# Decayed keys of a gated recurrence: turned on TensorE, or in 32x32 blocks on VectorE with 16 transfers per head

## The chip, the cores and the metric

One core of a Trainium2 chip runs the whole program in one launch. The metric is the device time of one execution in microseconds (us). Engines are called PE (TensorE; PEld is its weight load), DVE (VectorE), ACT (ScalarE), POOL (GpSimd) and SP (SyncE). All times on the profile are counted from the start of the span.

## The reference, cut to what matters

Two layers with RMSNorm and residual work on x of 512 x 1024 in float32. Layer 1 is an HGRN2 recurrence with 16 heads of 128 features, in chunks of 32 steps; layer 2 is dilated attention, and a final RMSNorm closes. The change touches layer 1 alone:

```python
q, f_pre, i_in, gate = u @ w_in        # four projections, 1024 -> 2048 each
f = lb + (1 - lb) * sigmoid(f_pre); k = 1 - f; b = cumsum(log f)     # in a chunk of 32
scores = causal((q * exp(b)) @ (k * exp(-b)).T)
o = scores @ v + (q * exp(b)) @ state
state = exp(b_last) * state + (k * exp(b_last - b)).T @ v
y = o * rsqrt(mean(o*o) + eps) * norm_g * silu(gate); h = x + y @ w_out
```

The kernel carries the state over blocks of 128 steps, of which there are four, so three blocks of keys decayed to the end of their block ("end-weighted keys", `kend`) are multiplied with the values.

## The kernel before, in words

Activations lie with features on the partitions and the 512 steps in the row. A large product is split in high and low parts of float32r: three matmuls of 512 columns for each block of 128 inputs (`split_matmuls`, L534). Weight tiles (512 KB) come through four slots: SP loads a tile once the slot's earlier tile has been split into its high part (ACT, `split_hi`, L955) and its low part (DVE, `split_lo`, L1342), each done when PE has finished the tile that held the slot (`load_after`, L365). Products land in three PSUM banks in turn.

Layer 1 goes over four quads of four heads (`quads`). In a quad PE works through three weight tiles for each head h: forget gate F, query Q and output gate G. Each tile is two halves of twelve 512-column matmuls. Between the halves the inner work of the head before is put in by a list (`recurrence`, called with `half` 0 to 5). For the last head of a quad it stands between the halves of the value products, or in the last quad between the columns of the out-projection. The order before is:

- after half 0, `scores`: 16 score products (L747, each two records), then, once `kend` is ready, the turning of `kend`: four products with the identity for block 1 (L752, each two records, into reversed strips of 32 partitions) and two transposes (L755) for blocks 0 and 2, into PSUM;
- after half 1, `updates`: three products of turned keys and values (L765), once ACT has copied PSUM to `kT` (`kT_copy`, L1110);
- after half 2, `outputs`: scores by values and state by queries (L776, L779), once DVE has masked the scores (L1493) and made the states (`states`, L1500 to L1503);
- after half 3, `norm_sum` (L786, L787): the sum of squares of the output, once ACT has squared it (L1115, L1117) and DVE has made its low part (`osq_low`, L1556).

DVE's order for head h is written out by hand in its `hg_body`: `gate` and `mask_scores` of the head before, the bound of F's exponent, `states` of the head before, `forget` (L1510), `cumulate` (L1518), `split_lo` of F, `osq_low` and `hg_output` (L1560, L1561) of the head before, then `decays` of this head: L1529 to L1550, with `kend` written at L1547 and signalled by `kend_ready`; then `split_lo` of Q, `y_low`, `bound_gate`, `split_lo` of G. ACT's order mirrors it: `kT_copy` of the head before, the sigmoid of F, `split_hi` of F, log (L1150), `square` of the head before, exp(b) (L1154), `out_rstd`, exp(-b) (L1158), `split_hi` of Q, `y_high`, exp of G (L1164), `split_hi` of G, `sigmoid` (L1132, L1134).

POOL first adds biases to a table for layer 2 (`bias_runs`, L453, 55 small instructions, with the value moves of the prologue, L444, in their middle), stores the table to DRAM and expands it there (L457 to L468), loads the first bias tiles (L430, L432), and only then enters `hg_body`, in which it moves value strips (`turn_chunks`, L444). In layer 2 POOL makes 16 transfers for each head to move 32x32 blocks between strips of partitions (`move_blocks`, L508), after DVE has turned them (L1754).

Of the kernel before, what the change touches and what calls it, by code (L numbers as in the profile page):

```python
# [30 lines left out]
F32 = mybir.dt.float32  # L31
# [101 lines left out]
def program(nc, x, ln_g, hg_w_in, hg_lb, hg_norm, hg_w_out, at_w_in, at_w_out, rel_bias, final_g,  # L133
            consts, classes, relmask, out):
    ctx = ExitStack()
    with ctx:
# [39 lines left out]
        rows = sb("rows", [P, 10, S])  # L176
        ef, fg, kk, lnf, bb, eb, enb, kend, spare_row, sT = [rows[:, i, :] for i in range(10)]

# [3 lines left out]
        aft = sb("aft", [P, S])  # L182
        kT = sb("kT", [P, ST - 1, P])
        state = sb("state", [P, ST - 1, P])
# [82 lines left out]
        q_ready, keys_ready, scores_done, sT_ready = sems("q_ready keys_ready scores_done sT_ready")  # L267
        kend_ready = sem("kend_ready")
        kT_done, kT_ready, U_done, state_ready = sems("kT_done kT_ready U_done state_ready")
        squared, osq_hi_ready, osq_ready = sems("squared osq_hi_ready osq_ready")  # L270
# [20 lines left out]
        def head(q, h):  # L291
            return q * HQ + h

        def quads(eng, body):
# [58 lines left out]
        def _(sp):  # L353
# [50 lines left out]
            for layer in (HG, AT):  # L404
                for n in range(layer.pro):
                    load_after(layer, None, n, False)

                def body(q, last):
                    for n in range(layer.quad_tiles(last)):
                        load_after(layer, q, n, last)  # L410
                quads(sp, body)

# [13 lines left out]
        def _(pool):  # L426
# [21 lines left out]
            for n, (g, bucket, first, count) in enumerate(runs):  # L448

                if n == len(runs) // 2:  # L450
# [3 lines left out]
                                              relb_sb[:, bucket * GROUPS + g:bucket * GROUPS + g + 1], None, ALU.add)  # L454
            ins.then_inc(ext_ready, 1)
            pool.wait_ge(ext_ready, 1)
            pool.dma_start(ext_dram.rearrange("g h e -> h g e"),  # L457
# [15 lines left out]
            load_bias(0)  # L473

            def hg_body(q, last):
                if not last:
                    turn_chunks(q)
            quads(pool, hg_body)

# [49 lines left out]
        def _(pe):  # L529
# [228 lines left out]
            def updates(g, h):  # L758

                if h == 0:  # L760
                    for turned in v_turned:
                        pe.wait_ge(turned, (g // HQ + 1) * 16 * NC)
                pe.wait_ge(kT_ready, g + 1)
                for b in range(ST - 1):
                    ins = nc.tensor.matmul(p_U[:, b * P:(b + 1) * P], kT[:, b, :], v_sb[0][:, b, h * P:(h + 1) * P],  # L765
                                           start=True, stop=True)
                ins.then_inc(U_done, 1)
# [32 lines left out]
            def hg_body(q, last):  # L800
                for h in range(HQ):
                    for half in range(2 * HG.per_head):
                        head_tile(HG, q, HG.per_head * h + half // 2, half % 2, first=(h == 0 and half < 2))
                        if h:
                            recurrence(head(q, h - 1), h - 1, half)
                for half in range(KT):
                    if last:
                        out_column(HG, q, HG.heads + half // 2, HG.heads + half, half, range(HQ - 1))
                    else:
                        values(HG, q, 0, half // 2, half % 2)  # L810
                    recurrence(head(q, HQ - 1), HQ - 1, half)
                out_projection(HG, q, last)
# [134 lines left out]
        def _(act):  # L947
# [160 lines left out]
            def kT_copy(g):  # L1108
                act.wait_ge(kT_done, g + 1)
                nc.scalar.activation(kT[:, :, :].rearrange("p a b -> p (a b)"), p_kT[:, 0:(ST - 1) * P], ACT.Copy)\  # L1110
                    .then_inc(kT_ready, 1)

            def square(g):
                act.wait_ge(O_done, g + 1)
                nc.scalar.activation(enb[:, :], p_O[:, :], ACT.Square).then_inc(squared, 1)  # L1115
                act.wait_ge(squared, g + 1)
                nc.scalar.activation(osq["hi"], enb[:, :], ACT.Copy).then_inc(osq_hi_ready, 1)  # L1117

# [17 lines left out]
            def hg_body(q, last):  # L1136
                for h in range(HQ):
                    g, before = head(q, h), head(q, h - 1) if h else None
                    number, bank, _ = HG.event(q, 3 * h + F_)
                    if h:  # L1140
                        kT_copy(before)
# [8 lines left out]
                    nc.scalar.activation(lnf[:, :], fg[:, :], ACT.Ln).then_inc(lnf_ready, 1)  # L1150
                    if h:
                        square(before)
                    act.wait_ge(b_ready, g + 1)
                    nc.scalar.activation(eb[:, :], bb[:, :], ACT.Exp).then_inc(eb_ready, 1)  # L1154
                    if h:
# [4 lines left out]
                    if h:  # L1160
                        y_high(before, h - 1)
# [8 lines left out]
                square(g)  # L1170
                if not last:
# [163 lines left out]
        def _(dve):  # L1335
# [184 lines left out]

            def decays(link, q, h, g, low_before):
                number, bank, _ = HG.event(q, 3 * h + Q_)
# [10 lines left out]
                if low_before:  # L1533
# [20 lines left out]
            def osq_low(g):  # L1554
                dve.wait_ge(osq_hi_ready, g + 1)
                nc.vector.tensor_tensor(osq["lo"], enb[:, :], osq["hi"].bitcast(F32), ALU.subtract).then_inc(osq_ready, 1)  # L1556

# [59 lines left out]
            def hg_body(q, last):  # L1617
# [9 lines left out]
                for h in range(HQ):  # L1627
                    g, before = head(q, h), head(q, h - 1) if h else None
                    if h:
                        gate(HG, q, h - 1, before, 3 * (h - 1) + G_)  # L1630
                        mask_scores(before)
# [12 lines left out]
                    early = last and h == HQ - 1  # L1644
# [17 lines left out]
                osq_low(g)  # L1662
                if last:
# [261 lines left out]
```

## Time and profile before

| | |
|---|---|
| median of 3 runs | 1588.45 us (1588.4 to 1588.81) |
| the profiled execution: its own time | 1588.76 us |
| its span, first to last instruction | 1587.1 us |
| around the span | 1.66 us |
| granted TensorE clock, mean | 0.999 of full |
| last `kend` product of layer 1 on PE | at about 492 us |

The profile gives busy time by engine, the chain that ended last, groups of instructions, and, on request, every instruction in order of time. In the timelines a row is the start in us, the length in us, the engine, the line, the operation and what it writes and reads, with a count where several are merged; idle time of the engine before it stands in brackets. Matmuls are pipelined, so the distance between two starts, not the length shown, is what a matmul takes from PE.

### The profile page before, as it was taken

What the parts mean: (1) busy time and instruction counts of PE and PEld (TensorE: products, weight loads), DVE (VectorE), ACT (ScalarE), POOL (GpSimd) and SP (SyncE); (2) the same over time, 40 slices, a digit from 0 to 9 for tenths busy, and PEclk for the clock granted to TensorE, in tenths of its full rate; (3) what the DMA queues carried; (4) which work ended last, traced back from release to release, by engine and by line L of the source; (5) the groups of instructions that cost most, each with busy time, mean ns of one, the idle gap of its engine ahead of it and who ended that gap; (6) DMA issues with size and microseconds to landing.
All of it is one profiled execution on the core that took longest, in us unless ns stands there. A gap on an engine that the chain in (4) does not pass through costs nothing.

```text
span 1587.1 us, 23898 instructions
## 1 busy us (share of the span) xinstructions
PE 1579.5 (100%) x8731; PEld 1306.9 (82%) x8731; DVE 807.4 (51%) x1415; ACT 633.3 (40%) x1078; POOL 360.2 (23%) x694
## 2 busy tenths in 40 slices
PE   9999999999999999999999999999999999999998
PEld 8888888888887888888888888888888888888887
DVE  7874675585577733444333444433245441434445
ACT  6553453454354533333232343322343332233333
POOL 5601000000000082222173211248022225502210
PEclk9999999999999999999999999999999999999999
DMA  6623223223321353444344433425344434534421
GB/s 194 201 80 112 79 79 106 81 78 99 100 73 48 120 152 98 111 106 112 91 140 114 117 93 97 104 91 165 86 106 112 116 78 132 144 89 110 111 73 67
DMA packets 268164, 169.23 MB, mean 107 GB/s; under 512 B 60032, under 2 KB 240848, under 8 KB 268080
## 3 DMA queue, kind: packets, MB, share of 16 engines
q1 hardware_dynamic: 204448, 138.75, 31.0%
q0 software_dynamic: 21488, 28.24, 5.9%
q10 hardware_dynamic: 42144, 1.05, 1.5%
q8 instruction: 61, 1.00, 0.3%
q14 instruction: 23, 0.19, 0.0%
HBM read 144.37 MB, written 5.71 MB: 95 GB/s over the span
## 4 chain that ended last, share of the span: by engine, by line
PE 99%; DVE 1%; ACT 0%; issue 0%; POOL 0%; ACTq 0%; POOLq 0%
PE proj L534 84%; PE inner L534 3%; PE inner L908 2%; PE inner L903 2%; PE inner L861 1%; PE inner L842 1%; PE inner L776 1%; PE inner L779 1%; PE inner L747 1%; PE inner L765 1%; PE inner L857 0%; PE inner L755 0%; PE proj L680 0%; PE inner L786 0%; PE inner L695 0%; PE inner L787 0%
## 5 line engine op out<-in xcount | busy, mean ns | idle before, releaser
L1342 DVE TENSOR_TENSOR w_lo<-raw,w_hi 128x1024 fp32r<-128x1024 f32 x252 | 307.3, 1220 | 476.3 <-ACT w_hi L955 473.1
L534 PE MATMUL proj<-u_hi,w_hi 128*128 128x512 f32 x1280 | 505.9, 395 | 0.2 <-issue 0.2
L534 PE MATMUL proj<-u_hi,w_lo 128*128 128x512 f32 x1280 | 498.9, 390 | 0.0
L534 PE MATMUL proj<-u_lo,w_hi 128*128 128x512 f32 x1280 | 498.8, 390 | 0.0
L955 ACT ACTIVATE w_hi<-raw 128x1024 fp32r<-128x1024 f32 x252 | 265.4, 1054 | 192.0 <-PE proj L534 131.3
L534 PEld LDWEIGHTS proj<-u_hi,w_hi 128*128 128x128 f32 x1280 | 240.4, 188 | 53.7 <-issue 5.0
L534 PEld LDWEIGHTS proj<-u_hi,w_lo 128*128 128x128 f32 x1280 | 240.2, 188 | 51.3
L534 PEld LDWEIGHTS proj<-u_lo,w_hi 128*128 128x128 f32 x1280 | 240.6, 188 | 48.2
L508 POOL DMA_DIRECT2D rows<-qx x240 | 117.7, 498 | 253.6 <-DVE qx L1754 251.3
L534 PE MATMUL proj<-w_hi,u_hi 128*128 128x512 f32 x440 | 173.6, 394 | 0.0
L534 PE MATMUL proj<-w_hi,u_lo 128*128 128x512 f32 x440 | 171.5, 390 | 0.0
L534 PE MATMUL proj<-w_lo,u_hi 128*128 128x512 f32 x440 | 171.3, 389 | 0.0
L1280 ACT ACTIVATE qk<-proj 128x512 f32<-128x512 f32 x96 | 57.0, 594 | 242.3 <-PE proj L534 242.3
L488 POOL DMA_DIRECT2D v<-qk x192 | 100.3, 529 | 55.5 <-PE inner L908 54.3
L1206 ACT ACTIVATE rows<-rows,negm 128x160 f32<-128x160 f32 (+2 forms) x128 | 56.7, 444 | 140.4 <-DVE negm L1714 140.4
L534 PE MATMUL proj<-y_hi,w_hi 128*128 128x512 f32 x248 | 97.1, 391 | 0.7 <-DVE sg L1479 0.4
L534 PEld LDWEIGHTS proj<-w_hi,u_hi 128*128 128x128 f32 x440 | 82.6, 188 | 17.6 <-DVE w_lo L1342 0.9
L534 PEld LDWEIGHTS proj<-w_hi,u_lo 128*128 128x128 f32 x440 | 82.6, 188 | 17.5
L534 PE MATMUL proj<-y_hi,w_lo 128*128 128x512 f32 x248 | 96.6, 389 | 0.0
L534 PEld LDWEIGHTS proj<-w_lo,u_hi 128*128 128x128 f32 x440 | 82.7, 188 | 16.8 <-issue 0.2
L534 PE MATMUL proj<-y_lo,w_hi 128*128 128x512 f32 x248 | 96.5, 389 | 0.0
L430 POOL DMA_DIRECT2D bias_n<-bias_tiles x16 | 9.0, 562 | 345.7 <-DVE rows L1704 335.2
(214 smaller groups left out, 1657.1 us busy)
## 6 DMA issues: line engine op xcount, KB each, us to landing
raw<-at_w_in SPq DMA_DIRECT2D x160, 512.0 KB, 4.3
raw<-hg_w_in SPq DMA_DIRECT2D x63, 512.0 KB, 4.0
rows<-qx POOLq DMA_DIRECT2D x240, 44.0 KB, 2.4
raw<-hg_w_out SPq DMA_DIRECT2D x16, 512.0 KB, 3.5
raw<-at_w_out SPq DMA_DIRECT2D x16, 512.0 KB, 5.1
v<-rows POOLq DMA_DIRECT2D x64, 64.0 KB, 2.3
v<-qk POOLq DMA_DIRECT2D x192, 16.0 KB, 3.4
v<-x SPq DMA_DIRECT2D x4, 512.0 KB, 6.3
```

What stands on the lines that cost most here:

```text
L488: pool.dma_start(v_sb[2][own:own + STEPS, r, :], staged(q, 2, s)[c * RES + r::CLASSES * RES, :]).then_inc(v_moved[s], 16)
L508: pool.dma_start(pT_far[j * CH:(j + 1) * CH, i, :, :], turned[i * CH:(i + 1) * CH, j, :, :])\
L534: ins = nc.tensor.matmul(bank[:, :], stationary(a), moving(b), start=(first and n == 0), stop=(last and n == 2))
L747: ins = nc.tensor.matmul(to, aft[:, b * P + c * CH:b * P + (c + 1) * CH], q_steps(b, 0, c, NC - c), start=True, stop=True)
L765: ins = nc.tensor.matmul(p_U[:, b * P:(b + 1) * P], kT[:, b, :], v_sb[0][:, b, h * P:(h + 1) * P], start=True, stop=True)
L776: ins = nc.tensor.matmul(p_O[:, s], v_sb[0][:, b, h * P:(h + 1) * P], sT[:, s], start=True, stop=(b == 0))
L903: nc.tensor.matmul(p_O[:, c * P:(c + n) * P].rearrange("p (t i n) -> p t i n", t=n, n=CH), v_sb[0][:, c, h * P:(h + 1) * P], tiles(2 * c, ...
L908: ins = nc.tensor.matmul(by_class[:, r], v_sb[c][:, r, h * P:(h + 1) * P], tiles(i, 1)[:, 0], start=False, stop=(i == len(TILES) - 1), ski ...
L955: nc.scalar.activation(w["hi"][:, slot, :], raw[:, slot, :], ACT.Copy).then_inc(hi_ready, 1)
L1206: nc.scalar.activation(probs[:, i, 0:n], probs[:, i, 0:n], ACT.Exp, bias=negm[:, i:i + 1], accum_out=stat[:, i // ST, 1, b:b + 1]).then_in ...
L1280: nc.scalar.activation(o, src, ACT.Copy, scale=QSCALE if i in (Q0, Q1, Q2) else 1.0)\
L1342: nc.vector.tensor_tensor(w["lo"][:, slot, :], raw[:, slot, :], w["hi"][:, slot, :].bitcast(F32), ALU.subtract).then_inc(w_ready, 1)
```

## The change: what it does

For 14 of the 16 heads (all but the last two of the last quad) DVE turns `kend` in 32x32 blocks (two transpose instructions, `turn_keys`), into a spare row of the work area. Sixteen transfers of 32 partitions x 384 B each then move the blocks to their strips of `kT`: eight from POOL's queue, eight from SP's. PE leaves out the eight L752 and two L755 records for these heads. `updates`, `outputs` and `norm_sum` are put one half later for them, and wait for both groups of transfers. `kT` is laid out with the three blocks innermost, so that the stationary operand of L765 is read with a step of three elements, for all 16 heads. The square goes to `tmp` in place of `enb`, exp(-b) goes ahead of the square on ACT, and on DVE `decays` and `split_lo` of Q go ahead of `hg_output`. POOL's part of layer 1 goes ahead of the storing of the bias table. For the last two heads the order is as before.

```diff
-        kT = sb("kT", [P, ST - 1, P])
+        kT = sb("kT", [P, P, ST - 1])
+        keys_of = lambda b: kT[:, :, b]
...
+        OWN_KEYS = 2
+        def by_transfer(last, h):
+            return not (last and h >= HQ - OWN_KEYS)
+        def square_of(transfer):
+            return tmp[:, 0, :] if transfer else enb[:, :]
+        def move_strips(eng, to, moved):
+            for c in to:
+                for i in range(NC):
+                    eng.dma_start(kT[c * CH:(c + 1) * CH, i * CH:(i + 1) * CH, :],
+                                  turned_keys[i * CH:(i + 1) * CH, c, :, :]).then_inc(moved, 16)
...
                     for n in range(layer.quad_tiles(last)):
                         load_after(layer, q, n, last)
+                        h = (n - SLOTS) // HG.per_head
+                        if layer is HG and n - SLOTS == h * HG.per_head and 0 <= h < HQ and by_transfer(last, h):
+                            wait_turn(sp, sp_met, keys_turned, head(q, h) + 1)
+                            move_strips(sp, range(NC // 2, NC), keys_high)
...
+            def move_keys(q, h):
+                wait_turn(pool, pool_met, keys_turned, head(q, h) + 1)
+                move_strips(pool, range(NC // 2), keys_low)
+            def hg_body(q, last):
+                for h in range(HQ):
+                    if by_transfer(last, h):
+                        move_keys(q, h)
+                if not last:
+                    turn_chunks(q)
+            quads(pool, hg_body)
             pool.wait_ge(ext_ready, 1)
...
-            def scores(g):
+            def scores(g, transfer):
...
                 ins.then_inc(scores_done, 1)
+                if transfer:
+                    return
                 pe.wait_ge(kend_ready, g + 1)
...
-                pe.wait_ge(kT_ready, g + 1)
+                if transfer:
+                    pe.wait_ge(keys_low, 8 * NC * NC * (g + 1))
+                    pe.wait_ge(keys_high, 8 * NC * NC * (g + 1))
+                else:
+                    pe.wait_ge(kT_ready, own_keys(g))
...
-            def recurrence(g, h, half):
+            def recurrence(g, h, half, transfer):
+                late = 1 if transfer else 0
                 if half == 0:
-                    scores(g)
-                elif half == 1:
-                    updates(g, h)
-                elif half == 2:
+                    scores(g, transfer)
+                elif half == 1 + late:
+                    updates(g, h, transfer)
+                elif half == 2 + late:
                     outputs(g, h)
-                elif half == 3:
+                elif half == 3 + late:
                     norm_sum(g)
...
                     nc.scalar.activation(enb[:, :], bb[:, :], ACT.Exp, scale=-1.0).then_inc(eb_ready, 1)
+                    if late:
+                        square(before, True)
                     split_hi(HG, q, 3 * h + Q_, last)
-                    if h:
+                    if late:
+                        out_rstd(before)
+                    if soon:
                         y_high(before, h - 1)
...
                     split_hi(HG, q, 3 * h + G_, last)
-                    if h == HQ - 1:
+                    if late:
+                        y_high(before, h - 1)
+                    if h == HQ - 1 and not by_transfer(last, h):
                         kT_copy(g)
                     sigmoid(g)
...
+            def turn_keys(g):
+                dve.wait_ge(kend_ready, g + 1)
+                blocks = kend.rearrange("p (b q n) -> p b q n", q=NC, n=CH)
+                nc.vector.transpose(turned_keys[:, :, :, 0:ST - 1:2].rearrange("p q n b -> p b q n"), blocks[:, 0:ST - 1:2, :, :])
+                last_first = bass.AP(turned_keys.tensor, turned_keys.offset + (NC - 1) * (ST - 1) * CH + 1,
+                                     [list(turned_keys.ap[0]), [-(ST - 1) * CH, NC], [ST - 1, CH]])
+                nc.vector.transpose(last_first, blocks[:, 1, :, :]).then_inc(keys_turned, 1)
...
                     .then_inc(kend_ready, 1)
+                if transfer:
+                    turn_keys(g)
...
                     if h:
-                        osq_low(before)
+                        osq_low(before, late)
+                    if soon:
                         hg_output(link, before)
...
-                    decays(link, q, h, g, early)
+                    decays(link, q, h, g, soon, by_transfer(last, h))
                     split_lo(HG, q, 3 * h + Q_, last)
-                    if h and h < HQ - 1:
-                        y_low(before, h - 1)
+                    if late:
+                        hg_output(link, before)
                     bound_gate(g)
                     split_lo(HG, q, 3 * h + G_, last)
-                    if h == HQ - 1 and not early:
+                    if late:
                         y_low(before, h - 1)
```

## Rows read from the trace of the kernel before

**Rows 1.** The page: busy time of the engines, and the chain that ended last.
```profile
PE 1579.5 (100%) x8731; PEld 1306.9 (82%) x8731; DVE 807.4 (51%) x1415; ACT 633.3 (40%) x1078; POOL 360.2 (23%) x694
...
PE 99%; DVE 1%; ACT 0%; issue 0%; POOL 0%; ACTq 0%; POOLq 0%
```

**Rows 2.** Timeline of PE, inner work of the first head, and the next scores.
```profile
54.38 0.77 PE L747 MATMUL inner<-qx,aft 128*32 128x128 f32 x32
54.96 0.40 PE L752 MATMUL inner<-ident,rows 128*32 128x128 f32 x8
...
55.49 0.48 PE L534 MATMUL proj<-u_hi,w_hi 128*128 128x512 f32 x1
...
58.35 0.83 PE L765 MATMUL inner<-v,kT 128*128 128x128 f32 x6
...
61.79 0.60 PE L776 MATMUL inner<-rows,v 128*128 128x128 f32 x4
...
66.12 0.39 PE L786 MATMUL inner<-osq_hi,ones_r 128*128 128x512 f32 x1
...
74.83 0.77 PE L747 MATMUL inner<-qx,aft 128*32 128x128 f32 x32
```

**Rows 3.** Timeline of PE in layer 2, products of 32-column tiles, then the projection.
```profile
602.75 0.86 PE L842 MATMUL inner<-qk 128*32 128x160 f32 x20
603.55 0.50 PE L534 MATMUL proj<-u_hi,w_hi 128*128 128x512 f32 x1
```

**Rows 4.** Timeline of DVE, between the first and the second head.
```profile
60.22 0.35 DVE L1503 SCALAR_TENSOR_TENSOR state<-state,tail,inner 128x128 f32<-128x128 f32 x1
61.19 0.55 DVE L1510 TENSOR_SCALAR rows<-rows,oml,lb 128x512 f32<-128x512 f32 x1 [0.62 <-ACT rows L1147]
...
62.52 1.22 DVE L1518 TENSOR_TENSOR_SCAN rows<-restart,rows 128x512 f32<-128x512 f32 x1 [0.33 <-ACT rows L1150]
...
64.85 0.69 DVE L1556 TENSOR_TENSOR osq_lo<-rows,osq_hi 128x512 fp32r<-128x512 f32 x1
...
69.68 0.68 DVE L1529 TENSOR_TENSOR qx<-proj,rows 128x512 f32<-128x512 f32 x1
...
73.66 0.68 DVE L1547 TENSOR_TENSOR rows<-aft,tail 128x512 f32<-128x512 f32 x1
```

**Rows 5.** Timeline of ACT, the square of the first head's output.
```profile
63.55 0.60 ACT L1115 ACTIVATE rows<-inner 128x512 f32<-128x512 f32 x1 [1.06 <-PE inner L779]
64.18 0.64 ACT L1117 ACTIVATE osq_hi<-rows 128x512 fp32r<-128x512 f32 x1
64.72 0.61 ACT L1154 ACTIVATE rows<-rows 128x512 f32<-128x512 f32 x1
```

**Rows 6.** Groups of DVE: the block transposes of layer 2.
```profile
L1754 DVE STREAM_TRANSPOSE qx<-rows 128x512 f32<-128x512 f32 x15 | 10.1, 670 | 0.0
```

**Rows 7.** Timeline of POOL: value moves, then bias additions.
```profile
36.68 4.13 POOL L444 DMA_DIRECT2D v<-qk  x8
40.85 16.63 POOL L453 TENSOR_SCALAR qk<-qk,bias_n 16x12 f32<-16x12 f32 x28
```

**Rows 8.** Landing of POOL's transfers: all 32 of L444.
```profile
DMA to landing us min/median/max: 1.8/1.9/6.1
```

**Rows 9.** Landing of the last five of L508 for one head, 688.9 to 690.9.
```profile
DMA to landing us min/median/max: 2.7/3.2/4.2
```

**Rows 10.** Timeline of SP in the prologue: issue of one transfer.
```profile
6.77 0.42 SPq L397 DMA_DIRECT2D rows<-hg_norm  x1
```

**Rows 11.** The page, DMA issues: layer 1's weight loads.
```profile
raw<-hg_w_in SPq DMA_DIRECT2D x63, 512.0 KB, 4.0
```

**Rows 12.** Lines L765 and L908: durations in ns, min, median, max.
```profile
L765 PEld LDWEIGHTS inner<-v,kT x96: 187/192/192, 58.1 to 494.8; 128*128 128x128 f32 x96
L765 PE MATMUL inner<-v,kT x96: 270/275/275, 58.4 to 494.9; 128*128 128x128 f32 x96
...
L908 PE MATMUL inner<-rows,v x256: 275/275/275, 664.1 to 1570.2; 128*128 128x128 f32 x128
```

More of the change, by code:

```diff
@@ L176, in program @@
         rows = sb("rows", [P, 10, S])
-        ef, fg, kk, lnf, bb, eb, enb, kend, spare_row, sT = [rows[:, i, :] for i in range(10)]
+        ef, fg, kk, lnf, bb, eb, enb, kend, turned_row, sT = [rows[:, i, :] for i in range(10)]
+        turned_keys = turned_row[:, 0:(ST - 1) * P].rearrange("p (q n b) -> p q n b", q=NC, n=CH)
         sq_sum = rows[:, 0, :]
@@ L268, in program @@
         kend_ready = sem("kend_ready")
+        keys_turned, keys_low, keys_high = sems("keys_turned keys_low keys_high")
         kT_done, kT_ready, U_done, state_ready = sems("kT_done kT_ready U_done state_ready")
@@ L292, in head, with own_keys @@
             return q * HQ + h
+        OWN_KEYS = 2
[8 more added lines that the diff above has]
+                                  turned_keys[i * CH:(i + 1) * CH, c, :, :]).then_inc(moved, 16)
+        def own_keys(g):
+            return g - (H - OWN_KEYS) + 1
         def quads(eng, body):
@@ L473, in _ @@
             load_bias(0)
[L475 to L478, printed above, removed]
             def move_classes(q, steps):
@@ L756, in scores, with updates @@
                 ins.then_inc(kT_done, 1)
-            def updates(g, h):
+            def updates(g, h, transfer):
                 if h == 0:
@@ L762, in updates @@
                         pe.wait_ge(turned, (g // HQ + 1) * 16 * NC)
-                pe.wait_ge(kT_ready, g + 1)
+                if transfer:
[3 more added lines that the diff above has]
+                    pe.wait_ge(kT_ready, own_keys(g))
                 for b in range(ST - 1):
-                    ins = nc.tensor.matmul(p_U[:, b * P:(b + 1) * P], kT[:, b, :], v_sb[0][:, b, h * P:(h + 1) * P],
+                    ins = nc.tensor.matmul(p_U[:, b * P:(b + 1) * P], keys_of(b), v_sb[0][:, b, h * P:(h + 1) * P],
                                            start=True, stop=True)
@@ L804, in hg_body @@
                         if h:
-                            recurrence(head(q, h - 1), h - 1, half)
+                            recurrence(head(q, h - 1), h - 1, half, by_transfer(last, h - 1))
                 for half in range(KT):
@@ L810, in hg_body @@
                         values(HG, q, 0, half // 2, half % 2)
-                    recurrence(head(q, HQ - 1), HQ - 1, half)
+                    recurrence(head(q, HQ - 1), HQ - 1, half, by_transfer(last, HQ - 1))
                 out_projection(HG, q, last)
@@ L1108, in kT_copy, with square @@
             def kT_copy(g):
-                act.wait_ge(kT_done, g + 1)
-                nc.scalar.activation(kT[:, :, :].rearrange("p a b -> p (a b)"), p_kT[:, 0:(ST - 1) * P], ACT.Copy)\
+                act.wait_ge(kT_done, own_keys(g))
+                nc.scalar.activation(kT[:, :, :].rearrange("p n b -> p b n"),
+                                     p_kT[:, 0:(ST - 1) * P].rearrange("p (b n) -> p b n", n=P), ACT.Copy)\
                     .then_inc(kT_ready, 1)
-            def square(g):
+            def square(g, transfer):
                 act.wait_ge(O_done, g + 1)
-                nc.scalar.activation(enb[:, :], p_O[:, :], ACT.Square).then_inc(squared, 1)
+                nc.scalar.activation(square_of(transfer), p_O[:, :], ACT.Square).then_inc(squared, 1)
                 act.wait_ge(squared, g + 1)
-                nc.scalar.activation(osq["hi"], enb[:, :], ACT.Copy).then_inc(osq_hi_ready, 1)
+                nc.scalar.activation(osq["hi"], square_of(transfer), ACT.Copy).then_inc(osq_hi_ready, 1)
             def out_rstd(g):
@@ L1138, in hg_body @@
                     g, before = head(q, h), head(q, h - 1) if h else None
+                    late, soon = h and by_transfer(last, h - 1), h and not by_transfer(last, h - 1)
                     number, bank, _ = HG.event(q, 3 * h + F_)
-                    if h:
+                    if soon:
                         kT_copy(before)
@@ L1150, in hg_body @@
                     nc.scalar.activation(lnf[:, :], fg[:, :], ACT.Ln).then_inc(lnf_ready, 1)
-                    if h:
-                        square(before)
+                    if soon:
+                        square(before, False)
                     act.wait_ge(b_ready, g + 1)
                     nc.scalar.activation(eb[:, :], bb[:, :], ACT.Exp).then_inc(eb_ready, 1)
-                    if h:
+                    if soon:
                         out_rstd(before)
                     nc.scalar.activation(enb[:, :], bb[:, :], ACT.Exp, scale=-1.0).then_inc(eb_ready, 1)
+                    if late:
+                        square(before, True)
                     split_hi(HG, q, 3 * h + Q_, last)
-                    if h:
+                    if late:
+                        out_rstd(before)
+                    if soon:
                         y_high(before, h - 1)
@@ L1169, in hg_body @@
                 g = head(q, HQ - 1)
-                square(g)
+                square(g, by_transfer(last, HQ - 1))
                 if not last:
@@ L1519, in cumulate, with decays @@
                     .then_inc(b_ready, 1)
-            def decays(link, q, h, g, low_before):
+            def turn_keys(g):
[5 more added lines that the diff above has]
+                nc.vector.transpose(last_first, blocks[:, 1, :, :]).then_inc(keys_turned, 1)
+            def decays(link, q, h, g, low_before, transfer):
                 number, bank, _ = HG.event(q, 3 * h + Q_)
@@ L1552, in decays, with osq_low @@
                     .then_inc(q_ready, 1)
-            def osq_low(g):
+            def osq_low(g, transfer):
                 dve.wait_ge(osq_hi_ready, g + 1)
-                nc.vector.tensor_tensor(osq["lo"], enb[:, :], osq["hi"].bitcast(F32), ALU.subtract).then_inc(osq_ready, 1)
+                nc.vector.tensor_tensor(osq["lo"], square_of(transfer), osq["hi"].bitcast(F32), ALU.subtract).then_inc(osq_ready, 1)
             def hg_output(link, g):
@@ L1628, in hg_body @@
                     g, before = head(q, h), head(q, h - 1) if h else None
+                    late, soon = h and by_transfer(last, h - 1), h and not by_transfer(last, h - 1)
                     if h:
@@ L1640, in hg_body @@
                     if h:
-                        osq_low(before)
+                        osq_low(before, late)
+                    if soon:
                         hg_output(link, before)
-                    early = last and h == HQ - 1
-                    decays(link, q, h, g, early)
+                    decays(link, q, h, g, soon, by_transfer(last, h))
                     split_lo(HG, q, 3 * h + Q_, last)
-                    if h and h < HQ - 1:
-                        y_low(before, h - 1)
+                    if late:
+                        hg_output(link, before)
                     bound_gate(g)
                     split_lo(HG, q, 3 * h + G_, last)
-                    if h == HQ - 1 and not early:
+                    if late:
                         y_low(before, h - 1)
@@ L1661, in hg_body @@
                     add_out(HG, q, HG.heads + 2, 2)
-                osq_low(g)
+                osq_low(g, by_transfer(last, HQ - 1))
                 if last:
```

## The prediction

> **What bounds the kernel now.** I read the page first: PE is busy for the whole span, 1579.5 of 1587.1 us, and the chain that ended last is PE for 99% [rows 1]. So only time taken off PE's own stream, or put into it, moves the end; work on the other engines counts where PE comes to wait for it. Next I read PE's timeline of one head's inner work, to get the price of what goes and the due time of what is put later [rows 2]; then DVE's and ACT's timelines of the same stretch, for how close each hand-over to PE is [rows 4, 5]; and last POOL, SP and the landing times, since these carry the new path [rows 7 to 11].
>
> **The change part by part.** I count time from a head's first score product S (54.38 us for the first head) [rows 2].
>
> What is removed: the turning of `kend` begins at 54.96 and the next projection starts at 55.49, so it takes 0.53 us of PE. Not all of it comes back. The scores are 32-column products, and a full 128x128 weight that follows such products waits for their end: in layer 2 the L842 group ends at 602.75 + 0.86 = 603.61 and the projection starts at 603.55, 0.06 before it [rows 3]. The last score product ends at 54.38 + 0.77 = 55.15 [rows 2], so without the turning the projection can start at about 55.08. The saving is 55.49 - 55.08 = 0.41 us per head, 14 x 0.41 = 5.8 us. The upper bound is the full 14 x 0.53 = 7.4 us. ACT's 14 copies of `kT` go as well; ACT is off the path.
>
> What moves: a half without inner work behind it takes (74.83 - 66.12 - 2 x 0.23 for the two sums)/3 = 2.75 us [rows 2]; the 0.23 is my estimate from that same spacing of 12 matmuls to a half. The due times on PE after the change are: updates at S + 3.97 - 0.41 + 2.75 = S + 6.31; outputs 3.44 later, S + 9.75; norm sum 4.33 later, S + 14.08; next scores at S + 20.45 - 0.41 = S + 20.04 [rows 2].
>
> The norm sum has a new squeeze. DVE makes `states` ahead of `forget`. The states end 60.57 - 58.35 = 2.22 us after the first update product, so at S + 8.53. Before, `forget` waited for ACT's sigmoid and not for the states [rows 4]; now it starts at S + 8.5. From it, the scan starts 1.33 later and ends 1.22 after that, S + 11.05 [rows 4]. ACT then makes exp(b) and exp(-b), 0.54 each by the spacing of its rows [rows 5], and squares from S + 12.1 (the output itself is there at 9.75 + 63.55 - 61.79 = S + 11.5). The low part ends 65.54 - 63.55 = 1.99 after the square's start [rows 4, 5], at S + 14.1, against 14.08 due. With the signal I take a wait of 0.1 us. It occurs where another head's forget work runs beside it, 3 + 3 + 3 + 2 = 11 heads: 1.0 us. Bounds: 0 and 0.3 us each (3.3 us), as each of some six hand-overs may differ by a few hundredths.
>
> The turn on DVE: two transposes of 384 columns together, at most the 0.67 us of the 512-column row [rows 6], 0.7 us with the wait for `kend`; its writes step by three elements, so up to 1.4. It lies on DVE, in front of the query's last step, the weight split and `hg_output`. The cover is that `decays` now starts at S + 14.1, right after `osq_low`, since `hg_output` stands behind it: `kend` is ready 74.34 - 69.68 = 4.66 later [rows 4], at S + 18.8, 1.3 us before the next scores, where it was ready 0.5 before them. If that cover were gone, each 0.1 would count 14 times.
>
> The transfers, for a common head: keys turned at S + 19.5, that is 0.6 to 0.7 us before the next scores S'. POOL issues eight transfers in 4.13 us, the last one starting some 3.6 us after the first [rows 7], at S' + 2.95. SP's eight take 0.42 each [rows 10], 3.4 us, and end sooner. A transfer of POOL's lands after 1.9 us in the median [rows 8], so at S' + 4.9, against S' + 6.31 due: 1.4 us to spare, no cost. The cover is gone if the last landing takes over 3.35 us. The weight load behind SP's eight starts 3.4 us later than it could; it takes 4.0 us [rows 11] and is wanted one round of four slots later, more than a head's 20 us: no cost. The bias table's DRAM traffic goes from the 60s of the span to behind the last moves, near 450 us, where its user is over 100 us away: no cost.
>
> The first head differs. POOL is in its bias additions until 40.85 + 16.63 = 57.48 us [rows 7], and the new moves stand behind them. Its eighth transfer then starts at 57.5 + 3.6 = 61.1, beside weight loads that SP had put off. With loads beside them the last moves of a head in layer 2 took 3.2 us in the median [rows 9]: landed at 64.3. PE is there at 54.38 + 6.31 = 60.7. The wait is 3.6 us, once. Bounds: 1.8 and 6.1 us of landing [rows 8], so waits of 2.2 and 6.5 us. Nothing later absorbs it, as PE has no slack elsewhere [rows 1].
>
> The last quad's hand-over from the moved to the old order: ACT must make y of head 14 of 16, its sigmoid, and only then the `kT` copy of the next head, which I work out to end just as PE asks for it. I take 0.2 us, bounds 0 and 1 us.
>
> The weights of L765 are now read with a step of three elements. The weight load shows 192 ns and the products 275, two records to a product [rows 12]. No row has a strided weight, so the bounds are 0 and a load that takes twice as long. The product spacing is (0.83 - 0.27)/5 = 0.11 us [rows 2]; adding 0.107 us to each of 96 records gives 10.3 us. I take 0, since the nearest row with an interleaved access of the same engine, the attention's L908, which writes PSUM at steps, shows the same 275 ns as L765 [rows 12]. The Trainium skill (SBUF — State Buffer, the note on SBUF cachelines) says that SBUF has 16-byte lines and that each access to a new line pays; a step of 12 bytes goes to a new line nearly every time, and by that rule the sum would be up to the 10 us worse. The same note says that non-contiguous PSUM access slows matmuls markedly, and by L908 the trace does not agree with that.
>
> **Sum**, against the profiled execution's own 1588.76 us: -5.8 + 3.6 + 1.0 + 0.2 = -1.0, so 1587.8. The median of the three runs is 0.3 below that execution, so I say 1587.5 us.
>
> **The rivals.**
> (a) Slower, the common head's keys come late: the mechanism is the landing of POOL's last transfer. It decides from 3.35 us on. The rows with weight loads beside reach 4.2 us [rows 9], which gives (4.2 - 3.35) x 13 = 11 us, 1598.5; at 3.7 it is 4.6 us, 1592. For it: rows of 384 B are shorter than any that these rows moved, and 16 transfers come at once from two queues. Against it: SP's own moves stand ahead of the next weight load, so POOL's last ones fly before it. Chance 0.13. The Trainium skill (DMA: Bandwidth & Descriptors, Specifications) puts the least size for full rate at 512 B, below which a transfer reads and writes back; no row here shows it.
> (b) Slower, the strided weights cost: full doubling gives 1598, half of it 1593. For it: nothing in the trace reads weights so. Against it: L908. Chance 0.12.
> (c) Faster: the full 0.53 comes back, or the norm sum never waits, and the first head's landing is 1.8: -7.4 + 2.2 = -5.2 gives 1583.3; with 0.41 it is -3.6, 1584.9. Chance 0.14.
> (d) Slower by a hold-up I have not found, such as DVE's doubled transpose or SP's late loads in the bias traffic, some 4 to 5 us. Chance 0.05.
> That the transposes on PE stay is excluded, since `scores` returns before them.
>
> **How the numbers follow.** The forecast has 0.56 and its own range is 1585 to 1591.5. A measurement of this kernel can tell about 0.2%, 3.2 us, from no change. Faster than 1585.3 is (c) with 0.14 and 0.07 of the forecast's lower tail: 0.21. Slower than 1591.6 is (a), (b) and (d), 0.30, less the cheap ends of them, 0.03: 0.27. The rest is 0.52. The range leaves out 0.06 below and some 0.12 above, the full forms of (a) and (b): 1584.3 to 1597.
>
> **What would show it.** In the changed profile: a projection start 0.70 us after the first score product; one PE wait of 2 to 6 us before the first L765 group, released by POOL's transfer; no wait, or under 0.1, at the other updates; waits of about 0.1 us at the norm sum; L765 spacing of 0.11 us. A spacing of 0.2 is (b); waits at all updates are (a). The saving is wrong if the start comes at 0.58.

## The result, and the profile after

The changed kernel is slower: 1598.05 us (median of 4 runs, 1597.27 to 1598.88) against 1588.51 us, a ratio of 1.006 with a 95% interval of 1.0042 to 1.0077. I had forecast 1587.5 us, no change, within 1584.3 to 1597. The sign of the forecast and the upper end of its range were both wrong. The profiled execution took 1598.88 us, 10.1 more than the one of before.

The page of the kernel after, span, busy time, and the shares of the chain that ended last:

```profile
span 1597.2 us, 23925 instructions
...
PE 1583.2 (99%) x8591; PEld 1311.8 (82%) x8591; DVE 813.8 (51%) x1443; ACT 627.7 (39%) x1064; POOL 415.5 (26%) x806
...
PE 91%; DVE 4%; ACT 1%; issue 1%; DMA 0%; SPq 0%; POOL 0%; DVEq 0%; ACTq 0%; POOLq 0%
```

PE leaves out 140 records and is yet busy 3.7 us longer; and the chain, 99% on PE before [rows 1], now leaves it for 9%. That share is not lost time: PE's waits of the whole span add up to 8.4 us, and the chain also runs through ACT and DVE where PE was busy. So there are two kinds of cost, longer PE work and new waits. The view of PE's waits names the second (who waited for whom: us in total, times, longest):

```profile
PE inner L805 <- DMA kT<-rows: 4.3, 2, 3.5
PE proj L568 <- DVE w_lo L1391: 2.7, 3, 0.9
```

PE's timeline of a common head (the third) answers to [rows 2]:

```profile
97.11 0.77 PE L781 MATMUL inner<-qx,aft 128*32 128x128 f32 x32
97.81 0.50 PE L568 MATMUL proj<-u_hi,w_hi 128*128 128x512 f32 x1
...
103.43 1.14 PE L805 MATMUL inner<-v,kT 128*128 128x128 f32 x6
...
107.14 0.60 PE L816 MATMUL inner<-rows,v 128*128 128x128 f32 x4
```

The projection starts 0.70 us after the first score product, as forecast, and the updates come at S + 6.32 with no wait. But the group of six update records is 1.14 us long, where it was 0.83 [rows 2], and outputs follow it by 3.71 us, not 3.44. A head's round, from one first score product to the next, is 20.35 us; it was 20.45 and I had expected 20.04.

With the starts of PE's inner work for all 16 heads in both traces, the 10.1 us come apart like this:

| where | us |
|---|---|
| turning left out, 14 heads, 0.39 each (20.45 to 20.06, the latter from the run with all repairs below) | -5.5 |
| longer update groups, 14 x 0.29 and 0.27 at the 15th head | +4.3 |
| value products wait for a weight tile, heads 4, 8 and 12 (updates at S + 7.49 instead of S + 6.32) | +3.5 |
| first head's round, 21.41 for 20.35 | +1.1 |
| 13th head's round, 26.70 for 20.35 | +6.4 |
| before the first scores: 55.34 for 54.38 | +1.0 |
| rest, behind layer 1 | -0.7 |

I put neither of the last two rows down to the change. Over the profiled executions of all kernels the first scores came between 54.34 and 55.34 us, with the 26 idle products of the start, which took 4.89 us in the one of before and 5.92 here. Behind the last head's scores every kernel below, also those that change nothing but a step of `kT`, shows 0.3 to 1.0 us less than that same execution of before. The last head pays nothing for its longer group: it has 1.20 us from the first update product to the next projection, where it had 1.21.

The largest item is the 13th head, the first of the last quad. Here are SP's timeline, two pieces of the chain that ended last (POOL passes its wait, then nothing that the profile shows), the timelines of POOL and PE, and the windows view with PE's granted clock as a share of full (the third figure from the end):

```profile
433.21 4.96 SPq L309 DMA_DIRECT2D kT<-rows  x8
438.28 1.16 SPq L386 DMA_DIRECT2D raw<-hg_w_in  x2
```

```profile
433.16 0.02 POOLq L325
433.17 3.46 issue
```

```profile
436.64 3.99 POOL L309 DMA_DIRECT2D kT<-rows  x8 [39.49 <-issue]
...
460.77 3.94 POOL L309 DMA_DIRECT2D kT<-rows  x8 [20.15 <-DVE rows L1577]
```

```profile
440.79 0.39 PE L568 MATMUL proj<-u_hi,w_lo 128*128 128x512 f32 x1
444.71 1.62 PE L805 MATMUL inner<-v,kT 128*128 128x128 f32 x6 [3.53 <-DMA kT<-rows]
445.98 0.77 PE L568 MATMUL proj<-u_hi,w_hi 128*128 128x512 f32 x1
446.56 0.63 PE L568 MATMUL proj<-u_lo,w_hi 128*128 128x512 f32 x1
446.98 0.63 PE L568 MATMUL proj<-u_hi,w_lo 128*128 128x512 f32 x1
```

```profile
444.00:451.00 7.00, 6.29 (x18) 5.26 (x19) 4.21 (x7) 1.78 (x3) 0.00 (x0) 0.51 0.00 0
```

SP starts its moves as soon as the keys are turned, at 433.2. POOL passes the same wait at 433.16 but starts its first transfer only at 436.64; the releaser is "issue", nothing that the profile shows. One head later the same step takes 0.6 us (460.21 to 460.77). It is not DVE's or SP's work beside it: at the fifth and ninth head, the first ones of their quads too, DVE has the same instructions in the same order and SP the same moves, and POOL starts at 181.47 and 307.57, 0.6 us after the keys are turned. POOL's last four transfers then fly beside the two weight loads that SP issues at 438.28, and take 3.8 to 4.4 us to land where its first four took 1.6. PE stands idle for 3.53 us, and from 444 to 451 us the granted clock is 0.51, the lower level of 1.2 GHz, where it was full before and after: 512-column products lie 0.43 us apart instead of 0.23. Of the 6.4 us, 3.7 are the wait and 2.7 the clock.

### The profile page after: what moved, and what is told of

Its sections match the earlier page's. It is cut to its first block, busy times and chain, and to the rows that moved or that the text cites. A ratio compares the mean times of both kernels' runs of the same rounds, so it can differ in the third digit from the quotient of the medians.

```text
span 1597.2 us, 23925 instructions
## 1 busy us (share of the span) xinstructions
PE 1583.2 (99%) x8591; PEld 1311.8 (82%) x8591; DVE 813.8 (51%) x1443; ACT 627.7 (39%) x1064; POOL 415.5 (26%) x806
## 4 chain that ended last, share of the span: by engine, by line
PE 91%; DVE 4%; ACT 1%; issue 1%; DMA 0%; SPq 0%; POOL 0%; DVEq 0%; ACTq 0%; POOLq 0%
PE proj L568 78%; PE inner L568 3%; PE inner L949 2%; PE inner L944 2%; PE inner L902 1%; PE inner L805 1%; PE inner L883 1%; DVE w_lo L1391 1%; PE inner L816 1%; PE inner L819 1%; PE inner L781 0%; PE inner L898 0%; DVE rows L1567 0%; DMA kT<-rows 0%; SPq L309 0%
## 5 line engine op out<-in xcount | busy, mean ns | idle before, releaser
L309 POOL DMA_DIRECT2D kT<-rows x112 | 56.7, 514 | 280.2 <-DVE rows L1577 240.3
```

The costliest lines, as they stand in the source:

```text
L309: eng.dma_start(kT[c * CH:(c + 1) * CH, i * CH:(i + 1) * CH, :], turned_keys[i * CH:(i + 1) * CH, c, :, :]).then_inc(moved, 16)
```

## The experiments

**The step of the weights, alone.** The kernel before, but `kT` has the blocks innermost:

```diff
-        kT = sb("kT", [P, ST - 1, P])
+        kT = sb("kT", [P, P, ST - 1])
...
-                    ins = nc.tensor.matmul(p_U[:, b * P:(b + 1) * P], kT[:, b, :], v_sb[0][:, b, h * P:(h + 1) * P],
+                    ins = nc.tensor.matmul(p_U[:, b * P:(b + 1) * P], kT[:, :, b], v_sb[0][:, b, h * P:(h + 1) * P],
```

> The kernel before with nothing changed but the layout of kT: ACT's copy writes it with the three blocks innermost, PE reads the stationary operand of the update products with a step of three elements. Stride theory (the step costs PE time by itself): the update group takes 0.90 us from its first product to the next projection where it took 0.58, so 16 x 0.32 = 5.1 us more, about 1593.6 us. Rival (the longer group comes of transfers in flight beside PE's reads, or of the waits before it): the group stays at 0.58 and the time at 1588.5.

Measured: 1593.01 us against 1588.86, ratio 1.0028 (1.0018 to 1.0037). From the group's first product to the next projection it is now 0.89 to 0.95 us, for all heads but the last. The stride theory holds; nothing in flight is needed for it. ACT's copy writes the new layout in all three kernels of this kind. Two more with other steps (blocks at `kT[:, b, :, 0]` of a tile with two elements to each key, and blocks innermost in a row of four) ask how the cost grows:

> The same with a step of two elements, 8 bytes. If what counts is a new 16-byte line at each read, a step of 8 bytes still has two reads to a line, and the group stays at 0.58 us. If any step costs, it is 0.7 or more.

> The same with a step of four elements, 16 bytes, so that each read is on a new line. Line theory: more than the 0.90 us of step three, about 1.0 to 1.2 us, that is 7 to 10 us in all. If any step costs the same, 0.90 us.

One run each: 1589.13 us with step two, 1599.81 with step four. The lines of the update's weight loads, in ns (min, median, max), with step two, three and four; with step one it is 192 [rows 12]:

```profile
L765 PEld LDWEIGHTS inner<-v,kT x96: 193/196/197, 58.3 to 495.5; 128*128 128x128 f32 x96
```

```profile
L765 PEld LDWEIGHTS inner<-v,kT x96: 251/261/263, 58.3 to 499.7; 128*128 128x128 f32 x96
```

```profile
L765 PEld LDWEIGHTS inner<-v,rows x96: 307/329/332, 58.8 to 506.7; 128*128 128x128 f32 x96
```

From the first product to the next projection it is 0.58, 0.61, 0.90 and 1.19 us for steps one to four; with step four nine of the heads show 1.35 to 1.43, and why is not shown (`kT` lies in the work area there). A step of 8 bytes is almost free, 12 and 16 are not. The Trainium skill (SBUF — State Buffer, the note on SBUF cachelines) says that full speed wants two accesses to a 16-byte line, and the trace agrees: with step two there are two, with three 1.33, with four one. Over the six records, 0.90 and 1.19 us are 0.05 and 0.10 more for each, which goes with the longer weight loads.

**The changed kernel without the step.** Turned keys and `kT` block by block, so that a transfer moves three runs of 128 B per partition:

```diff
-        turned_keys = turned_row[:, 0:(ST - 1) * P].rearrange("p (q n b) -> p q n b", q=NC, n=CH)
+        turned_keys = turned_row[:, 0:(ST - 1) * P].rearrange("p (q b n) -> p q b n", q=NC, n=CH)
...
-        kT = sb("kT", [P, P, ST - 1])
-        keys_of = lambda b: kT[:, :, b]
+        kT = sb("kT", [P, ST - 1, P])
+        keys_of = lambda b: kT[:, b, :]
```

> The changed kernel with kT and the turned keys laid out block by block: PE reads with step one again, and each transfer moves three runs of 128 B per partition instead of one of 384 B. Stride theory: 5.1 us less, about 1593, with the update group back at 0.58 us. Rival: the shorter runs make the transfers land later, by over 1.3 us, and PE waits before every update, which would give the 5 us back or more.

Measured: 1597.78 us (1593.74 to 1602.6, 6 runs), ratio 1.0052 (1.0035 to 1.007). The group is back at 0.58 us and the common round is 20.07, so the PE part came as expected. The third head's transfers from POOL land after 1.6 to 2.1 us with either run length: the rival fell. But the median hardly moved, and the runs lie 9 us apart. The profiled one, 1600.48, shows why; waits of PE, then POOL's timeline at the first head:

```profile
PE inner L805 <- DMA kT<-rows: 9.7, 2, 5.9
```

```profile
53.60 4.26 POOL L478 TENSOR_SCALAR qk<-qk,bias_n 16x1 f32<-16x1 f32 x5
57.81 4.41 POOL L309 DMA_DIRECT2D kT<-rows  x8
```

Here POOL was in its bias additions until 57.8, in the profiled execution of the changed kernel until 56.3. Its transfers began at 57.81, the last three met SP's weight loads and landed after 3.3 to 5.0 us, and PE waited 5.9 us at the first head with a fall of the clock behind it. Whether the first head costs 1.1 or 7.5 us hangs on a microsecond of POOL's.

**The split of the weight tile.** In the last head of a quad, DVE makes `hg_output` after the split of G's tile:

```diff
-                    if late:
+                    if late and h < HQ - 1:
                         hg_output(link, before)
                     bound_gate(g)
                     split_lo(HG, q, 3 * h + G_, last)
+                    if late and h == HQ - 1:
+                        hg_output(link, before)
```

> The changed kernel, but for the last head of a quad DVE bounds the gate and splits the weight tile of G ahead of hg_output. Theory of the late split: PE's waits for DVE's w_lo in the value products (three, 1.2 us each with their shift) go, 3.5 us in all; updates of heads 4, 8 and 12 of 16 come 6.3 us after their scores where they come 7.5. Rival (the tile is late since its load is late behind SP's transfers): the waits stay.

Measured: 1595.01 us, ratio to before 1.0035 (1.0022 to 1.0049), 3.0 less than the changed kernel. PE's and DVE's timelines in the changed kernel, then DVE's with the repair:

```profile
119.44 0.39 PE L568 MATMUL proj<-w_hi,u_lo 128*128 128x512 f32 x1
120.73 0.50 PE L568 MATMUL proj<-w_hi,u_hi 128*128 128x512 f32 x1 [0.90 <-DVE w_lo L1391]
```

```profile
117.61 0.68 DVE L1620 TENSOR_TENSOR y_f<-inner,rstd 128x512 f32<-128x512 f32 x1
118.45 0.75 DVE L1621 SCALAR_TENSOR_TENSOR y_f<-y_f,param,sg 128x512 f32<-128x512 f32 x1 [0.15 <-DVE y_f L1620]
119.12 0.42 DVE L1532 TENSOR_SCALAR eg<-eg 128x512 f32<-128x512 f32 x1
119.45 1.22 DVE L1391 TENSOR_TENSOR w_lo<-raw,w_hi 128x1024 fp32r<-128x1024 f32 x1
```

```profile
117.84 1.22 DVE L1391 TENSOR_TENSOR w_lo<-raw,w_hi 128x1024 fp32r<-128x1024 f32 x1
118.97 0.69 DVE L1620 TENSOR_TENSOR y_f<-inner,rstd 128x512 f32<-128x512 f32 x1
```

The value products of the first 128 steps use all four weight tiles within two halves, so the tile that is split once G's products are done (at 114.4) is wanted at 119.67, 5 us later; between heads it is three tiles later, some 17 us. In the changed kernel it is done at 120.67, and PE goes on at 120.73. With the repair it is done at 119.06, ahead of 119.44 + 0.23. The waits are gone and the updates of heads 4, 8 and 12 stand at S + 6.32 like the common ones: the theory of the late split holds, and SP's late loads had no part in it.

**POOL's first transfer behind its loop.** A dummy transfer at the start of the last quad's code:

```diff
             def hg_body(q, last):
+                if last:
+                    pool.dma_start(warm[:, :], ones[0:CH, 0:(ST - 1) * CH]).then_inc(warmed, 16)
                 for h in range(HQ):
```

> The changed kernel, and POOL issues one small transfer of constants into a spare tile at the start of its last quad's code, ahead of the wait for the first keys of that quad. Theory of first use (the 2.9 us that POOL loses there between the passed wait and its first transfer come with the first transfer instruction after the loop): the dummy takes them while POOL is idle, the group of eight follows the wait by 0.6 us, PE's wait of 3.5 us at the 13th head's updates falls under 0.7 us and the clock stays up: 6 us less. Rival (the delay comes with the wake after the wait, or from what DVE or the DMA engines do at that time): it stays, and so do the 6 us.

Measured: 1592.04 us (10 runs), ratio to before 1.0019 (1.001 to 1.0028), 6.0 less than the changed kernel. POOL's timeline:

```profile
395.14 1.97 POOL L471 DMA_DIRECT2D v<-qk  x4 [7.80 <-ACT qk L1016]
399.95 0.50 POOL L491 DMA_DIRECT2D warm<-ones  x1 [2.85 <-issue]
433.67 4.02 POOL L311 DMA_DIRECT2D kT<-rows  x8 [33.22 <-DVE rows L1581]
```

The 2.85 us have moved to the dummy, which waits for nothing, 34 us before they could hurt. The eight follow the turned keys by 0.6 us, PE does not wait and the clock stays at full. So it is not the wake after the wait that costs the time: in this kernel the delay goes with the first transfer instruction behind the loop. It is not tied to that place, as the kernel with nine and seven shows below. What POOL does in that time, such as fetching its code, no row shows; the view of DMA has no packet of the instruction queues from 432 to 440 us in the changed kernel, nor from 397 to 400 in this one.

**The bias additions.** Their second half behind all key moves:

```diff
+            for r in runs[:len(runs) // 2]:
+                add_bias(*r)
+            turn_chunks(None)
...
             quads(pool, hg_body)
+            for r in runs[len(runs) // 2:]:
+                ins = add_bias(*r)
+            ins.then_inc(ext_ready, 1)
```

> The changed kernel, but the second half of POOL's bias additions (28 small instructions, 16 us) comes after the moves of all keys. Theory: the first head's transfers start at 55.2 and not at 56.7 us, and PE's wait of 0.9 us at the first updates goes: 1 us less in the run profiled, more where that wait grows until the clock falls. The bias table is still ready some 80 us ahead of its use. Rival: the wait is set by SP's transfers or by the loads that land beside them, and stays.

Measured: 1598.62 us (4 runs), no gain over the changed kernel; the first updates still come 0.9 us later than S + 6.32. So the theory fell where it was tested. POOL's and SP's timelines:

```profile
55.87 4.17 POOL L309 DMA_DIRECT2D kT<-rows  x8 [14.89 <-DVE rows L1579]
```

```profile
55.37 5.04 SPq L309 DMA_DIRECT2D kT<-rows  x8
```

POOL is early now, and its last transfer lands at 61.16. SP's eight take 5.04 us, the last lands at 61.62, and PE starts at 61.76: the wait was SP's. SP spends 0.63 us on such a transfer, not the 0.42 of [rows 10].

**All four repairs.**

> All four in one: keys block by block, the early split for the last head of a quad, the dummy transfer, the late bias additions. If the three waits and the step of the weights are all that the change costs, what is left is 14 x 0.39 = 5.5 us saved: 1583.3 us against 1588.8. If there is a cost that I have not found, it is above 1585.

Measured: 1584.02 us (1583.59 to 1584.29, 6 runs) against 1589.07, ratio 0.9968 (0.9956 to 0.998). It beats both kernels. Waits of PE, the only one left from the transfers:

```profile
PE inner L811 <- DMA kT<-rows: 0.9, 1, 0.9
```

The round is 20.06 us for every moved head after the first. The saving of 5.5 and the first head's 1.1 make -4.4; measured is -5.05, so the list of costs is closed within a microsecond, and nothing of size is left unfound. The six runs lie within 0.7 us. Whether that needs the late bias additions was not tried; they are the repair that brought nothing alone.

**Nine and seven.** On top of that, POOL takes nine of a head's transfers and SP seven:

```diff
-                            move_strips(sp, range(NC // 2, NC), keys_high)
+                            move_strips(sp, STRIPS[9:], keys_high)
...
-                move_strips(pool, range(NC // 2), keys_low)
+                move_strips(pool, STRIPS[:9], keys_low)
```

> The kernel with all four repairs, and POOL issues nine transfers of a head, SP seven. SP's issues lie 0.6 us apart and POOL's 0.5, so theory (the wait left at the first head, 1.0 us, is SP's eighth issue): it falls by 0.5 us or so and the time is 1583.5 us; if POOL's were the last to land, the wait grows by 0.3 us. No other head changes. The difference to the kernel with eight and eight can hardly be told in the times, only in the profile.

Measured: 1605.32 us (4 runs), ratio 1.0102 (1.0085 to 1.0119): 21 us worse than eight and eight, against my expectation. PE's waits, then SP's and POOL's timelines and the landings of POOL's last two transfers at the third head:

```profile
PE inner L811 <- DMA kT<-rows: 16.2, 13, 3.0
```

```profile
103.31 0.39 SPq L388 DMA_DIRECT2D raw<-hg_w_in  x1
```

```profile
99.03 4.83 POOL L311 DMA_DIRECT2D kT<-rows  x9 [15.23 <-DVE rows L1583]
```

```profile
DMA to landing us min/median/max: 1.8/2.8/3.9
```

The eighth lands after 1.8 us and the ninth, issued at 103.31, the moment SP issues its weight load, after 3.9. In twelve of the fourteen moved heads it is the same: eight transfers after 1.6 to 2.0 us and the ninth, issued within 0.4 us of a load, after 3.3 to 4.1. At the second head the load came 0.25 us behind the ninth, which landed after 2.3, and PE did not wait. In the kernel with eight and eight, SP issues the load of the third head at 100.69, 1.1 us after POOL's last transfer (99.55), too late to meet it. That the load and not the number nine is to blame rests on that second head and on the same lengthening where POOL's fifth to eighth met a load, at the 13th head of the changed kernel, and its sixth to eighth, at the first head of the one without the step; a ninth with no load near it was not tried.

Of the 21 us, 16.2 are these waits and 3.4 two falls of the clock, behind the waits of 2.6 us (first head) and 3.0 us (12th). The rest is mostly some 0.1 us behind each wait, where the group has 0.67 to 0.69 us to the next projection and not 0.59. The 12th is another case. POOL's timeline there, and at its dummy transfer:

```profile
377.82 2.73 POOL L311 DMA_DIRECT2D kT<-rows  x5 [16.98 <-DVE rows L1583]
382.45 2.16 POOL L311 DMA_DIRECT2D kT<-rows  x4 [1.90 <-issue]
```

```profile
407.22 1.96 POOL L471 DMA_DIRECT2D v<-qk  x4 [7.75 <-ACT qk L1018]
409.16 0.50 POOL L490 DMA_DIRECT2D warm<-ones  x1
```

POOL stops for 1.90 us in the middle of its nine, with no wait between them, and the four behind the stop meet the load and land after 3.4 to 4.2 us. The dummy behind the loop, which came 2.85 us late in the two kernels above that have it, starts at once. So the hold-up is not bound to the end of the loop: with one more transfer in the loop it is inside it. Its cause stays open.

## Why the prediction was wrong, point by point

- **The saving** was sized right: 0.41 forecast, 0.39 measured (20.45 to 20.06), and the projection starts at S + 0.70.
- **The strided weights** are one step that failed. "I take 0, since the nearest row ... shows the same 275 ns" leant on a row of PSUM writes to judge SBUF reads of the stationary operand. The price was within my bounds (0 to 10.3): 4.3 us. As rival (b) I gave it 0.12. The weight load became 69 ns longer, where the upper bound had it take twice its 192 ns.
- **The weight tiles** are the second: the sum has no term for `split_lo` of G, which the new order puts behind `hg_output`. I had noted that the turn stands in front of a split and had named no one who waits for it. "Wanted one round of four slots later, more than a head's 20 us: no cost" was said of SP's loads, and no wait for a weight tile came of them; for the split it does not hold where the value products take four tiles at once. Measured: 3.5 us.
- **The common head's transfers** were right for 8 and 8: they landed in time. The spare was 1.2 us for the 1.4 forecast, in part by luck: at the third head the keys were turned 1.0 us before the next scores and not 0.6, and POOL's first transfer came 0.6 us after that, which I had left out. Rival (a)'s mechanism, a weight load beside POOL's last transfers, is real: it is at the 13th head, and nine and seven shows it at thirteen heads of fourteen. What kept it away is the reason that I gave against it, SP's own moves standing ahead of the load; the margin was 1.1 us.
- **The 13th head** is the third and largest, 6.4 us, and was not in the prediction at all. I took each moved head to start its transfers when its keys are turned; here POOL came 2.9 us later than elsewhere, and the load and the clock made 6.4 of it. Rival (d), the hold-up not found, had 0.05.
- **The first head** was 3.6 forecast, 1.1 measured. POOL was free at 56.3, not 57.5, its transfers landed after 1.7 and not 3.2, and SP's issues of 0.63 us set the end. That is under my lower bound of 2.2. The kernel without the step, 5.9, lies inside the bounds, by the mechanism that I had named.
- **The norm sum's** squeeze (1.0 us) and the last quad's hand-over (0.2) did not show: no wait at either.

In sum, from the forecast of -1.0: plus 4.3, 3.5 and 6.4, less 2.5 at the first head and 1.2 for the squeezes, plus 0.3 for the saving (5.5, not 5.8) and 0.3 of the execution's own (+1.0 and -0.7), which gives +10.1.

## What to carry to other kernels

Let the stationary operand's elements lie in steps of at most two float32: a layout made for longer runs in the transfers can cost PE more than it saves, and here the longer runs saved nothing. When transfers are made to replace PE work, look for the odd places, the first pass, the last one behind a loop, and the spot where weights are taken faster than elsewhere; the common head was right here, and every loss but the step was at such a place. Place small urgent transfers so that no large load is issued with them. Where the trace shows an engine held up with no wait, move harmless work to that place, and look for the place again after each change of that engine's program: the dummy that paid here met no hold-up in the next kernel.

## What the runs showed of the hardware that I had not expected

- POOL was held up with nothing that the profile shows: its first transfer behind the loop began 3.5 us after its wait had been passed, where 0.6 is common, or 2.85 us after the work before it where it had no wait. In the kernel with nine and seven it was 1.90 us between the fifth and sixth transfer of one head, in the loop, and nothing behind it.
- A 12 KB transfer of POOL's landed after 1.6 to 2.2 us with no load issued near it and after 3.3 to 5.0 us when a 512 KB load of SP's was issued with it or just before. Runs of 128 B and of 384 B per partition landed alike. The Trainium skill (DMA: Bandwidth & Descriptors, Specifications) asks for 512 B for full rate. Both lie under that, but POOL's value moves, 64 KB with runs of 2 KB, landed no sooner (1.8 us at best [rows 8]), so at this size the landings show no such cost.
- SP's transfers between partitions lay 0.63 us apart, POOL's 0.50 to 0.54; SP spent 0.39 us on issuing a weight load of 512 KB.
- With 3.5 us of idle time the granted clock of PE fell, and stood at 0.51, the lower of its two levels, for about 7 us. With nine and seven it fell with the waits of 2.6 and 3.0 us as well (0.76 on average from 64 to 71 us, 1.00 again from 68), and not with the one of 1.5. The falls cost 1.5 to 2.7 us on top of the waits. The 1.5 was with the longest wait, of 5.9 us, where a part of the slow stretch lay in the wait itself.
